# First stage in place, modulation products as rows, attention units in one sequence, later modulation on GpSimd, merge over eight banks

## The reference

```python
shift, scale, gate = split(silu(c) @ mod_mix_w + b, 3)          # one row c per request
h = rmsnorm(x, g) * (1 + scale) + shift
q, k, v, rx, rg, ga, gb = split(h @ w_in)
attn = band_attend(q, k, v, bias)        # 64-token chunks, 8 past chunks, clipped relative bias
rnn  = rg_lru(conv4(rx)) * gelu(rg)
merged = sigmoid(ga) * (attn @ w_branch[:512]) + sigmoid(gb) * (rnn @ w_branch[512:])
x = x + gate * (merged @ w_out)
shift, scale, gate = split(silu(c) @ mod_ffn_w + b, 3)
h = rmsnorm(x, g2) * (1 + scale) + shift
val, gt = split(conv3(h @ ffn_up_w));  x = x + gate * ((val * gelu(gt)) @ ffn_down_w)
y = rmsnorm(x, final_g)
```

## Time and profile before

| | us |
|---|---|
| three runs | 3130.22, 3130.86, 3138.67 (median 3130.86) |
| the profiled execution | 3139.11 |
| its span in the profile | 3137.3, granted clock 0.949 |
| busy in it | PE 2824.1 (90%), DVE 1703.4, ACT 1281.5, POOL 131.3 |

### The profile page before, as it was taken

How to read it: one execution, slowest core, us unless ns; L and a number is a source line. 1 busy time by engine, 2 the same in 40 slices (tenths; PEclk the granted TensorE clock), 3 DMA queues, 4 the chain that set the end, 5 groups by cost and what they waited for, 6 DMA issues and landing times.

```text
span 3137.3 us, 50876 instructions
## 1 busy us (share of the span) xinstructions
PE 2824.1 (90%) x19176; PEld 1898.3 (61%) x19176; DVE 1703.4 (54%) x3112; ACT 1281.5 (41%) x2406; POOL 131.3 (4%) x90
## 2 busy tenths in 40 slices
PE   6468999999986688977789899999999999999998
PEld 5224666666655567743369856666666666666665
DVE  2664645464544456655557776677767666311112
ACT  1564646464643345511135554545454544200000
POOL 0220000000001000000002110000000000000000
PEclk9889999999996789888899999999999999999999
DMA  5221221222163332224455411111111115522221
GB/s 198 66 68 49 69 88 67 91 67 91 67 171 79 98 64 89 96 95 164 157 137 140 118 49 54 54 54 55 67 54 54 54 60 199 174 72 80 86 65 37
DMA packets 204911, 282.18 MB, mean 90 GB/s; under 512 B 56144, under 2 KB 156496, under 8 KB 200032
## 3 DMA queue, kind: packets, MB, share of 16 engines
q1 hardware_dynamic: 194848, 268.79, 27.0%
q10 hardware_dynamic: 8848, 8.74, 0.8%
q0 software_dynamic: 1072, 2.65, 0.2%
HBM read 193.31 MB, written 89.46 MB: 90 GB/s over the span
## 4 chain that ended last, share of the span: by engine, by line
PE 72%; DVE 10%; ACT 5%; DMA 5%; issue 4%; SPq 2%; ACTq 0%; DVEq 0%
PE ps L2281 60%; PE ps L2366 3%; DMA merged<-arena 2%; PE ps L2355 2%; PE ps L2344 2%; PE ps L2258 2%; PE ps L2229 2%; DVE arena L1806 1%; DVE arena L1995 1%; DVE arena L1552 1%; ACT arena L851 1%; ACT arena L1230 1%; SPq L551 1%; DMA arena<-in_w_mod 1%; DMA arena<-in_w_mod_rest 1%
## 5 line engine op out<-in xcount | busy, mean ns | idle before, releaser
L2281 PE MATMUL ps<-arena 128*128 128x352 f16 (+1 forms) x15048 | 2096.7, 301 | 28.5 <-ACT arena L963 10.9
L2281 PEld LDWEIGHTS ps<-arena 128*128 128x128 f16 x15048 | 1413.2, 97 | 712.9 <-issue 22.9
L2433 PE MATMUL ps<-arena 128*128 128x512 f16 (+1 forms) x960 | 197.7, 370 | 61.6 <-DVE arena L1918 59.0
L2175 DVE SCALAR_TENSOR_TENSOR arena<-ps,arena 128x352 f32<-128x352 f32 (+1 forms) x64 | 29.9, 490 | 350.6 <-PE ps L2281 301.2
L1290 ACT ACTIVATE arena<-ps 128x352 f32<-128x352 f32 x264 | 119.7, 464 | 199.3 <-PE ps L2281 199.3
L2433 PEld LDWEIGHTS ps<-arena 128*128 128x128 f16 x960 | 85.2, 103 | 174.2 <-issue 64.8
L1466 ACT ACTIVATE arena<-arena 128x352 f32<-128x352 f32 x48 | 23.9, 498 | 407.3 <-DVE arena L2175 407.3
L2002 DVE SCALAR_TENSOR_TENSOR arena<-arena 128x512 f16<-128x512 f32 x154 | 103.8, 689 | 128.2 <-ACT arena L1254 128.2
L2344 PE MATMUL ps<-arena 128*128 (+4 forms) x480 | 100.2, 331 | 81.0 <-DVE arena L1831 78.7
L2366 PE MATMUL ps<-arena 128*128 (+3 forms) x1200 | 163.0, 285 | 1.9 <-DVE arena L1850 1.9
L2366 PEld LDWEIGHTS ps<-arena 128*128 128x128 f32 (+2 forms) x1200 | 159.4, 208 | 3.6 <-issue 3.0
(11 more groups left out here) (196 smaller groups left out, 2752.8 us busy)
## 6 DMA issues: line engine op xcount, KB each, us to landing
arena<-in_w_up SPq DMA_DIRECT2D x44, 512.0 KB, 3.8
ffn_hidden<-arena SPq DMA_DIRECT2D x44, 512.0 KB, 3.3
arena<-ffn_hidden SPq DMA_DIRECT2D x5, 3872.0 KB, 18.9
arena<-in_x_cols SPq DMA_DIRECT2D x24, 704.0 KB, 4.6
arena<-gates SPq DMA_DIRECT2D x8, 2112.0 KB, 10.2
arena<-in_w_proj SPq DMA_DIRECT2D x32, 512.0 KB, 4.4
gates<-arena SPq DMA_DIRECT2D x16, 1024.0 KB, 8.2
arena<-in_w_mod_rest SPq DMA_DIRECT2D x32, 512.0 KB, 3.3
```

The lines of the kernel that those rows point to most:

```text
L2281: mm = pe.matmul(out, wt[:, k, wp, :], act_t[:, k, hp], start=(first and k == 0 and n == 0), stop=(last and k == K - 1 and n == 2), skip_g ...
L2433: mm = pe.matmul(out, wt[:, wp, k, :], mixT[:, k, hp, t:t + w], start=(k == k0 and m == 0), stop=(k == k1 - 1 and m == 2))
```

## The change

- **First stage.** SP loads two column groups, three lots of modulation weights (4 tiles each), the value weights, the last lot, then four more column groups. The column groups have six buffers and are modulated in place. `modulation` now holds the two columns of silu(c) as weights and moves 512 columns of `mod_mix_w` at a time, 32 float32 matmuls in all; ACT copies the rows out and PE turns them back into columns with 16 small transposes. The work of a pass is cut in two lots: A (the four parts that need no sum) of pass p is followed by B (the four of POOL's sums) of pass p-1.
- **Attention.** One sequence of 136 units without loops: unit g+1's scores, unit g-1's transposes, unit g-2's outputs, across the pairs. `heads_in` of the next pair but one waits for `o_filled` alone. 
- **Later modulation.** Tiles 0 to 21 go to POOL: two products of 1024 and seven halving additions each (`ada_tile`, 9 instructions), with two tile buffers; DVE sums the last eight partial sums of each in one instruction. Tiles 22 to 31 stay on DVE, two to an f for f = 0 to 4, and the first of them waits until POOL has done all of its own. POOL splits the cached keys of pairs 0 and 1 first, those of pairs 2 and 3 ahead of tiles 5 and 10.
- **Merge.** Four pairs of banks instead of two (PE waits for the step four back), the product of the recurrent half first, and one product pulled ahead of the last attention outputs. DVE's low part of a step comes after the sum of the next step. The first merge loads are issued during the last pair.

```diff
-MW_LOTS = [(0, 6), (6, 12), (12, 16)]
+NX = 6
...
+        xr = [at_(37888 + CE * KT * i, 8 * CE).rearrange("p (k t) -> p k t", k=KT) for i in range(NX)]
...
+        ADA_POOL = 22
+        ADA_MERGE = (2, 2, 2, 2, 2, 0, 0, 0)
+        ADA_SP = [2, 7, 12, 18, ADA_POOL] + [ada_before(f + 1) for f in range(KT)]
...
             def later_tile(n):
-                if n:
-                    sp.wait_ge(dm_used, n)
-                sp.dma_start(dmw, a["w_mod_rest"][n]).then_inc(dmw_loaded, 16)
+                if n == 1:
+                    sp.wait_ge(th_stored[0], 32 * KT)
+                if n >= 2:
+                    sp.wait_ge(dm_used, n - 1)
+                sp.dma_start(dmw[n % 2], a["w_mod_rest"][n]).then_inc(dmw_loaded[n % 2], 16)
...
+            for j in range(NJ):
+                if j == NJ - 1:
+                    for k in range(NJ):
+                        sp.dma_start(mixT[:, NJ + k], rnn_d[k]).then_inc(mix_loaded, 16)
+                    sp.wait_ge(o_filled, NUNIT * (NJ - 1))
+                    merge_tile(0)
+                    merge_tile(1)
+                if j + 1 < NJ:
+                    if j >= 1:
+                        sp.wait_ge(o_filled, NUNIT * j)
+                    heads_in(j + 1)
+                    cached_keys(j + 1)
+                for n in range(ADA_SP[j], ADA_SP[j + 1]):
+                    later_tile(n)
...
+            def ada_tile(n):
+                pool.wait_ge(dmw_loaded[n % 2], 48 + 16 * (n // 2))
+                pool.wait_ge(kc_ready, min(NJ, 2 + n // 5))
...
+                pool.tensor_tensor(djunk[:, 0], dmw[n % 2], crowv[:, 0], ALU.mult).then_inc(ada_step, 1)
+                pool.tensor_tensor(djunk[:, 1], dmw[n % 2], crowv[:, 1], ALU.mult).then_inc(ada_step, 1)
+                for w in (512, 256, 128, 64, 32, 16, 8):
+                    pool.wait_ge(ada_step, step)
...
+                    pool.tensor_tensor(out, djunk[:, :, 0:w], djunk[:, :, w:2 * w], ALU.add).then_inc(ada_step, 1)
...
                 for k in range(KT):
-                        mm = pe.matmul(ps[:, 0, 2 * f:2 * f + 2], mw[:, f, k, :], csv[:, k, :],
+                    mm = pe.matmul(ps[0:2, 4 + g, :], csv[:, k, :], mw[:, 4 * g:4 * g + 4, k, :],
...
+            def merge_product(g, m):
+                f, (t, w) = g // 5, BLOCKS[g % 5]
+                keep_above_zero(pe, d_dve, 2 * g - 6)
+                product(ps[:, 2 * (g % 4) + m, 0:w], w, 4 * m, 4 * m + 4, dsp[f % 2], t)
...
                     dve.tensor_tensor(mrg[:, b, 0:w], sig[:, b, 0, 0:w], sig[:, b, 1, 0:w], ALU.add)
+                    if g:
+                        merged_lo(g - 1)
                     if n == 1 and f + 1 < KT:
                         merge_lo(f + 1)
-                    dve.wait_ge(d_mhi, g + 1)
-                    dve.scalar_tensor_tensor(mstage[:, 1, t:t + w], mrg[:, b, 0:w], 0.5 / WS, ...)
-                    if n < ADA_MERGE[f]:
-                        ada_tile(ada_before(f) + n)
+                    if 1 <= n <= ADA_MERGE[f]:
+                        if f == 0 and n == 1:
+                            dve.wait_ge(ada_step, ADA_OPS * ADA_POOL)
+                        ada_tile(ada_before(f) + n - 1)
```

More of the change, by code:

```diff
@@ L522, in _ @@
                         sp.wait_ge(p_filled, 1)
+                        for b in range(2):
+                            sp.wait_ge(v_stored[b], 16 * VST[b])
                     else:
@@ L912, in _ @@
                     n += 1
+            for c in B_ORDER:
+                high0(NE - 1, c)
             def proj_hi(r, c):
@@ L1897, in merge_lo, with out_lo @@
+            def out_lo(x):
+                t = slice(x.q0, x.q0 + x.rows)
+                dve.wait_ge(ot_hi, x.tile + 1)
+                dve.scalar_tensor_tensor(mixT[:, x.j, 1, t], ps[:, 7, 0:x.rows], XS, mixT[:, x.j, 0, t],
+                                         ALU.mult, ALU.subtract).then_inc(ot_ready, 1)
             def merge_lo(f):
@@ L2236, in sum_squares0 @@
                     pe.wait_ge(n_std, e - 1)
-                pe.matmul(ps[:, 1 + e % 2, 0:CE], ones, nacc, start=True, stop=True).then_inc(n_ss, 1)
-            for e in range(3):
-                sum_squares0(e)
-            for g in range(3):
-                mm = modulation(g)
-            mm.then_inc(mod_filled, 1)
+                pe.matmul(ps[:, 1 + e % 2, 0:CE], ones, sq0[:, 0], start=True, stop=True).then_inc(n_ss, 1)
+            sum_squares0(0)
+            modulation(0)
+            sum_squares0(1)
+            for g in range(1, 4):
+                modulation(g)
+                modulation_columns(g - 1)
+            modulation_columns(3).then_inc(mod_filled, 1)
             def value_tile(n):
@@ new lines, in scores @@
+            def scores(x):
+                if x.i == 0:
+                    pe.wait_ge(at_loaded[x.b], 240 * (x.j // 2) + 240)
+                if x.sample:
+                    pe.wait_ge(kc_ready, x.j + 1)
+                keep_above_zero(pe, s_added, x.u - 1)
+                for bank, c in ((0, min(x.w, 512)), (1, x.w - 512)):
+                    if c <= 0:
+                        continue
+                    k = x.k0 + 512 * bank
+                    for m, kk in enumerate((khh[x.b], kll[x.b])):
+                        mm = pe.matmul(ps[0:x.rows, 2 * x.h + bank, 0:c], qs[x.b][:, x.h, x.q0:x.q0 + x.rows],
+                                       kk[:, x.h, k:k + c], start=(m == 0), stop=(m == 1))
+                mm.then_inc(s_filled, 1)
@@ new lines, in outs @@
+            def outs(x):
+                pe.wait_ge(t_act, x.u + 1)
+                keep_above_zero(pe, t_dve, wide(x.u + 1))
+                keep_above_zero(pe, o_ready, x.u)
+                nk = (x.w + P - 1) // P
+                for c in range(nk):
+                    k = min(P, x.w - c * P)
+                    mm = pe.matmul(ps[0:x.rows, 6, 64 * x.h:64 * x.h + 64], pt[0:k, x.h, c * P:c * P + x.rows],
+                                   vv[x.b][0:k, x.v0 + c, 64 * x.h:64 * x.h + 64],
+                                   start=(c == 0), stop=(c == nk - 1))
+                mm.then_inc(o_filled, 1)
```

656 lines of the change are left out of this document (301 added, 355 removed).

## The result

The kernel after takes 2965.1 us (median of four runs, 2961.1 to 2967.0), the kernel before 3132.3 us (median of the four runs beside them). The ratio is 0.946, with a 95% interval of 0.944 to 0.948: 167 us less. The forecast was 2938 us, within 2893 to 2990.

A forecast was written before the change was run, and what follows sets the result against it. It took DVE to be nearest full in the first stage, PE to bound attention, and the `mstage` store the merge. -62 - 110 + 2 - 23 = -193 from 3139.1 gave 2946, lowered to 2938 for the median; range 2893 to 2990.

The forecast's parts named there:

- First stage, -62: Before the projections: small matmuls removed and passes of 22.8 us, so the stage takes 211 us for 272.7.
- nothing waits any more for the low parts of its own sums, so I take DVE's whole work: First stage: a pass lasts DVE's work of 21.8 us plus 1 of handing over, 22.8 for 27.2.
- Attention, -110: First scores to first merge product: four pairs without later-modulation tiles or drains between them, 318 us for 428.
- The loops' removal I cost at nothing: PE has no gap in them: Attention: unrolling the loops itself gains nothing; full units stay at 2.51 us.
- Later modulation, +2: 22 tiles on POOL at 10.9 us each, done at 337 us, cost about 2 us; upper bound +45.
- stall seen by PE about 2: Start of the merge: DVE's wait for POOL costs PE about 2 us, as PE is three steps ahead.
- Merge, -23: Merge: a cycle of 31 us for 34 to 35, so the output projection starts at 236 for 259.
- a merge bound by PE, -75: Merge's bound: PE sets the pace, 8 x 22 us; as a rival, 2888 us, 6%.
- The slower case: Attention: POOL and DVE take turns, a unit lasts about 9 us instead of 2.5, +221, 3159 us; 4%.
- The 10 us for four tiles: Attention's last pair before the change: four later-modulation tiles of 2 x 1.24 us took some 10 of its 91.3.

The follow-up runs named there:

- heads_before_tiles: The kernel after, with SP loading three and five later-modulation tiles ahead of the heads' operands of pairs 2 and 3, instead of five and five: 2942.3 us.
- the two runs behind it: The kernel after with the 22 tiles on DVE: each tile's two instructions two units apart, 2987.9 us; or whole tiles with eight filler matmuls each on PE, 2995.4 us.
- the undone order: The kernel after with the low part of a merge step directly behind its sum, as before the change, and four pairs of banks: 2987.9 us.
- the stores in two parts: The kernel after, with a merge tile's first 1024 tokens stored behind its third step and the rest at its end: 2918.4 us.
- the three best edits: Single edits to the kernel after: value stores ahead of SP's waits, 2940.3 us; heads' operands before later tiles, 2942.3 us; merge stores in two parts, 2918.4 us.

## Why the prediction was right, and where it was not

The measured 2965 lies in the range, 27 us above the forecast, and that is in part luck. The sum missed the profiled executions by 15 us (-193 against -178), and its terms missed by more: the first stage by +24, attention by +5, the wait for POOL by about +10, the merge by about -20 (the two stages taken as unchanged gave back 3.5). The other 12 us lie between profiled executions and medians: the forecast took 8 off, and the profiled execution of after was itself 4 us below its median.

- **First stage, -62: measured -38.** Modulation starts at 57 us, as forecast (55). The step that failed is "nothing waits any more for the low parts of its own sums, so I take DVE's whole work": SP still waited for those sums, and the value stores were queued behind it. The forecast had read SP's order for the loads and not for the stores. The run with the stores in front gives back 22.7 of the 23.8 us. (Its first pass still took 27 us, in part for the reason in the last rows below; the stage's end made that up.)
- **Attention, -110: measured -105,** with two errors that nearly cancel. "The loops' removal I cost at nothing: PE has no gap in them" was wrong: the profile shows no gap, and yet two units take 4.57 us for 5.01, with the same durations of their matmuls, which over the 88 units that were in loops is 19 us. Whether it was the loop that cost the 0.22 us a unit, or the older order of the units' work, was not tried alone. Against it stand the wait for the bias (9.0 us, and 4 more at the lower clock behind it: the pair took 87.5 us, and 74.7 in heads_before_tiles), which the forecast missed though it had counted SP's queue for POOL's pauses, and short units of 1.98 us (worked out from a pair's 74.8) where it had 1.8.
- **Later modulation, +2: about +12.** POOL was done 351 us after the first scores and not 337: it began its tiles 48 us in, not 45; 22 tiles at 11.14 us and not 10.9 lost 5; from one lot of tiles to the next, keys included, it took 28.8 and 27.7 us, not 26; and two of the last tiles began 0.8 and 1.7 us late. The wait of DVE that resulted is 11.5 us. The step that failed is its price, "stall seen by PE about 2": the merge goes from store to store, so what delays the first store delays all. Without the wait the first store is issued 29.3 us in for 41.7, and the merge takes 215.8 us for 227.6 (217.6 and 214.8 in the two runs behind it). By the figure of the Trainium skill ("GPSIMD Engine Reference", section 3.1) a tile was an estimate of 9.0 us, which led the other way; the measured 11.14 decides for the rows.
- **Merge, -23: measured -31 with that wait in it, -43 without it.** The mechanism held, shown by the undone order: 4.4 us a cycle. The term was sized too small, since a cycle takes 28.5 us and not 31. Too long were the weights' halves (2.0 us with their wait, not 3) and the store's flight (12.0, not 12.7). The bound that the forecast gave for a merge bound by PE, -75, is what the stores in two parts reach (181 us, -78).
- **The slower case** (POOL and DVE taking turns in attention) is refuted by the score additions, 737 ns in both. Where DVE reads SBUF twice they do take turns, in the merge's first steps as shown above and in the first stage: with the stores in front, the three additions of a sum of squares took 4.64 us beside POOL's sums and 1.82 alone.

```profile
70.92 4.64 DVE L1596 TENSOR_TENSOR arena<-arena 128x704 f32<-128x704 f32 x3
...
79.88 1.82 DVE L1596 TENSOR_TENSOR arena<-arena 128x704 f32<-128x704 f32 x3
```

The Trainium skill ("SBUF — State Buffer", "SBUF: two separate sides") names, among the VectorE instructions that take turns with GpSimd, those with two SBUF inputs. The rows here agree: the additions of the squares have two, the score addition has one.

- **The 10 us for four tiles** in the last pair, taken from their duration of 2.5 us each, about held. On PE's timeline of before, the eight units beside those tiles lasted 25.7 us from scores to scores (1263.46 to 1289.19); the same eight of the last pair in heads_before_tiles, without tiles, lasted 16.1 (1118.33 to 1134.44). That is 9.6 us less, a part of it from the new order of the units. The 4.3 us a tile of the run with tiles on DVE belong to full units, where a wait on PE costs its length and then the clock.

## What to carry to other kernels

For each engine that issues DMAs, read what each transfer stands behind, the stores as much as the loads: two of the three best edits only moved DMA issues ahead of a wait that they did not need. Where one staging buffer sets a cycle, store its first half as soon as it is written; here PE became the bound by it, so that a second buffer, which was not tried, could have given little more. Price a stall on TensorE at its length and the slower matmuls behind it, and prefer two short stalls to one long.

## What the hardware showed that was not expected

- A single idle gap of 1.82 us on TensorE was followed by 3.9 us at a granted clock of 0.56, and the clock fell at 11 of 12 such gaps; behind the gaps of 0.56 and 0.67 us shown above it stayed at 1.00. Eight more matmuls at each of the 22 tiles made the kernel 36 us faster.
- On GpSimd a product of 1024 elements took 2.35 us, 2.3 ns an element; the seven halvings of 2032 elements together took 6.08, 3.0 ns an element.
- GpSimd, busy for 78 of 84 us in the last stretch of attention, changed the score additions of VectorE, which read PSUM and SBUF, by nothing that the profile can show.
